# A hybrid encoder trunk on one core: projection groups computed by halves of the tokens, and the differential rotation done by VectorE's shuffle

## The reference, cut to what matters

```python
def apply_partial_rope(x, cos, sin):
    r = cos.shape[-1]                       # 8 of a head's 64 features
    x1, x2, rest = x[..., :r], x[..., r:2 * r], x[..., 2 * r:]
    return jnp.concatenate([x1 * c - x2 * s, x2 * c + x1 * s, rest], axis=-1)

def diff_mixer(q, k, v, ...):
    q = apply_partial_rope(rms_norm(q.reshape(b, t, 8, 64), q_head_g), cos, sin)
    k = apply_partial_rope(rms_norm(k.reshape(b, t, 8, 64), k_head_g), cos, sin)
...
    u = rms_norm(h, attn_norm_g[l]) @ w_in[l]      # 40 groups of 128 columns
```

## Time and profile before

| | |
|---|---|
| median of 3 runs | 2256.19 us (2255.35 to 2264.37) |
| the profiled execution, its own time | 2260.73 us |
| its span, first to last instruction | 2258.9 us |
| mean granted TensorE clock | 0.975 |
| TensorE matmul busy | 2062.5 us (91%) |
| VectorE, ScalarE, GpSimd busy | 1063.1, 820.8, 993.5 us |

### The profile page before, as it was taken

One profiled execution on the slowest core, in us unless ns is written; L12 is line 12 of the kernel. 1 busy time (PEld: TensorE's weight loads), 2 busy tenths in 40 slices (PEclk: granted clock), 3 DMA queues, 4 the chain that ended last, 5 costly groups with the idle time before them and its releaser, 6 DMA issues.

```text
span 2258.9 us, 32608 instructions
## 1 busy us (share of the span) xinstructions
PE 2062.5 (91%) x13298; PEld 1781.2 (79%) x13298; DVE 1063.1 (47%) x1653; ACT 820.8 (36%) x1344; POOL 993.5 (44%) x593
## 2 busy tenths in 40 slices
PE   7989998888778999999999999997877789999999
PEld 7978887567657999999989878884555567888887
DVE  8532355565664744442038332555655656444400
ACT  3322343576554222222224322443664633222221
POOL 4455432784311444444434454335861334444444
PEclk9999999999998999999999999999998999999999
DMA  4211111000001222233222111111000012333333
GB/s 161 66 56 57 57 46 67 10 1 19 29 12 37 85 94 87 91 94 94 94 85 84 57 57 57 48 38 56 1 7 31 19 56 94 94 94 98 97 103 112
DMA packets 40035, 143.79 MB, mean 64 GB/s; under 512 B 4432, under 2 KB 4560, under 8 KB 39760
## 3 DMA queue, kind: packets, MB, share of 16 engines
q1 hardware_dynamic: 39888, 141.72, 19.6%
HBM read 139.60 MB, written 2.10 MB: 63 GB/s over the span
## 4 chain that ended last, share of the span: by engine, by line
PE 72%; DVE 11%; ACT 8%; issue 6%; POOL 2%; DMA 1%; SPq 0%; ACTq 0%; DVEq 0%; POOLq 0%
PE pb L850 44%; PE pb L885 6%; PE pb L886 6%; PE pb L887 6%; ACT ebuf L1468 2%; PE pb L1287 1%; DVE rowmax L1926 1%; POOL parts L632 1%; PE pb L1295 1%; ACT rstd L1436 1%; PE pb L1227 1%; DVE proj L1858 1%; PE pb L987 1%; ACT ebuf L1479 1%; ACT parts L1524 1%
## 5 line engine op out<-in xcount | busy, mean ns | idle before, releaser
L632 POOL TENSOR_TENSOR parts<-raw,parts 128x1024 fp32r<-128x1024 f32 x248 | 602.5, 2430 | 829.0 <-ACT parts L1524 828.8
L850 PE MATMUL pb<-mix,parts 128*128 128x264 f32 x4608 | 670.7, 294 | 41.1 <-POOL parts L632 15.7
L850 PEld LDWEIGHTS pb<-mix,parts 128*128 128x128 f32 x4608 | 609.2, 193 | 68.0 <-issue 26.1
L1524 ACT ACTIVATE parts<-raw 128x1024 fp32r<-128x1024 f32 x248 | 262.5, 1058 | 851.1 <-PE pb L850 549.6
L850 PE MATMUL pb<-proj_r,parts 128*128 128x264 f32 x3104 | 429.2, 286 | 0.5 <-POOL parts L632 0.5
L850 PEld LDWEIGHTS pb<-proj_r,parts 128*128 128x128 f32 x3104 | 401.2, 189 | 0.8 <-issue 0.7
L885 PE MATMUL pb<-proj_r,parts 128*128 128x512 f32 x528 | 207.5, 393 | 0.8 <-DVE mbuf L1858 0.8
L887 PE MATMUL pb<-proj_r,parts 128*128 128x512 f32 x528 | 207.7, 393 | 0.0
L886 PE MATMUL pb<-proj_r,parts 128*128 128x512 f32 x496 | 198.1, 399 | 0.0
L1864 DVE TENSOR_TENSOR h<-h,pb 128x528 f32<-128x528 f32 (+1 forms) x48 | 33.2, 693 | 274.9 <-PE pb L850 143.9
L1858 DVE TENSOR_TENSOR mbuf<-pb,rstd 128x528 f32<-128x528 f32 (+1 forms) x44 | 30.8, 700 | 214.8 <-PE pb L850 110.5
(11 more groups left out here) (277 smaller groups left out, 2831.6 us busy)
## 6 DMA issues: line engine op xcount, KB each, us to landing
raw<-w_stream SPq DMA_DIRECT2D x250, 512.0 KB, 3.5
w_head<-w_heads SPq DMA_DIRECT2D x8, 512.0 KB, 4.9
h<-x_t SPq DMA_DIRECT2D x8, 264.0 KB, 6.8
out_t<-h SPq DMA_DIRECT2D x8, 256.0 KB, 4.7
con<-consts SPq DMA_DIRECT2D x1, 1652.5 KB, 10.5
par<-params SPq DMA_DIRECT2D x1, 340.0 KB, 4.3
con<-consts SPq DMA_DIRECT2D x1, 128.0 KB, 7.1
```

Source lines behind the costliest of these rows:

```text
L632: nc.gpsimd.tensor_tensor(parts[:, n % PARTS, 1, :], w, parts[:, n % PARTS, 0, :].bitcast(FP32), ALU.subtract).then_inc(split.sem, 1)
L850: last = nc.tensor.matmul(pb[rows_, 2 * p + a, 0:HALF], lhs_t, rhs[:, a * HALF:(a + 1) * HALF], start=start, stop=stop)
L1524: nc.scalar.activation(parts[:, n % PARTS, 0, :], raw[:, r % RAW, :], ACT.Copy).then_inc(lead_ready.sem, 1)
```

## The change

Both parts touch slots 0 to 99 alone, in both layers.

By halves: a group's 48 matmuls keep their number, but the 24 of the first half of the tokens come first (slots 4n, 4n+1), then the 24 of the second (4n+2, 4n+3). VectorE scales each half out by its own instruction (128x264): the first at slot 4n+2, ahead of that slot's jobs, the second at the next boundary. A boundary's first piece waits for the first half of the group before, slot 4n+2 for its second.

Rotation: `perm_d` is no longer multiplied. At the norm's slot VectorE shuffles the scaled tile into `BM` (`stream_shuffle`, 32 partitions at a time, the first two eights swapped). At `turned` it multiplies `BM` by the sines in place, and the sum with GpSimd's cosine product comes at the next slot, as the job `roped`. The sign goes into the sine table once, at group 6 of layer 0.

```diff
+TURNED_AT = ((1, 64), (2, 68), (3, 72), (4, 76), (6, 82), (7, 86), (9, 92), (10, 97))
-               + [(slot, "turned", j) for j, slot in ((1, 64), (2, 68), ...])
+               + [(slot, "turned", j) for j, slot in TURNED_AT] + [(slot + 1, "roped", j) for j, slot in TURNED_AT])
...
 GpSimd, cosines
-                pool.wait_ge(rs_used.sem, rs_used.at(l, j + 1))
-                pool.wait_ge(rot_ready.sem, rot_ready.at(l, t + 1))
+                pool.wait_ge(swapped.sem, swapped.at(l, t + 1))
...
 TensorE
+            def half_piece(l, g, a, k0):
+                n = l * N_SLOT + g
+                if k0 == 0 and a == 0:
+                    pe.wait_ge(split.sem, n + 1)
+                    if g == G_SSD:
+                        pe.wait_ge(evac.sem, evac.at(l, g))
+                    else:
+                        pe.wait_ge(half_evac.sem, half_evac.at(l, g - G_SSD))
+                elif k0 == 0:
+                    pe.wait_ge(evac.sem, evac.at(l, g))
+                o, cut = pb[:, 2 * bank_pair(g) + a, 0:HALF], slice(a * HALF, (a + 1) * HALF)
+                for k in range(k0, k0 + KD // 2):
+                    w_lead, w_rest = (parts[:, n % PARTS, b, k * P:(k + 1) * P] for b in range(2))
+                    lead, rest = (ap[:, cut] for ap in xg_parts(k))
+                    nc.tensor.matmul(o, w_lead, lead, start=(k == 0), stop=False)
+                    nc.tensor.matmul(o, w_lead, rest, start=False, stop=False)
+                    last = nc.tensor.matmul(o, w_rest, lead, start=False, stop=(k == KD - 1))
+                if k0:
+                    done = w_used if a else half_done
+                    last.then_inc(done.sem, 1)
...
-            def turned(l, j):
-                pe.wait_ge(log_ready.sem, log_ready.at(l, RS_N + j + 1))
-                pe.wait_ge(rs_used.sem, rs_used.at(l, j + 1))
-                product(2, C("perm_d"), tile_of(proj, DQ + NORMS[j][1]), True, True).then_inc(rot_ready.sem, 1)
...
-                    k = (KD // PIECES) * (p % PIECES)
-                    beside(l, G_SSD + p // PIECES, 0, xg_parts, ((k, k + KD // PIECES),))
+                    half_piece(l, G_SSD + p // PIECES, p % PIECES // 2, KD // 2 * (p % 2))
...
 VectorE, norm
+                if what == "d":
+                    dve.wait_ge(rs_used.sem, rs_used.at(l, j + 1))
+                    dve.wait_ge(roped.sem, roped.at(l, t))
+                    nc.vector.stream_shuffle(tile_of(proj, BM), tile_of(proj, tile), SWAP).then_inc(swapped.sem, 1)
 VectorE, turned
-                nc.vector.tensor_tensor(halves(sines), pair(2), halves(C("sin_d")), ALU.mult).then_inc(rot_used.sem, 1)
+                link(nc.vector.tensor_tensor(sines, sines, C("sin_d"), ALU.mult))
+            def sines_added(l, j):
                 dve.wait_ge(qcos.sem, qcos.at(l, t + 1))
+                nc.vector.tensor_tensor(tile_of(proj, DQ + t), tile_of(proj, DQ + t), tile_of(proj, BM), ALU.add).then_inc(roped.sem, 1)
...
                     if p % PIECES == 0 and p:
-                        scale_out(l, g, tile_of(proj, TILE_AT[g]))
+                        scale_half(l, g, 1, tile_of(proj, TILE_AT[g]))
+                    if p % PIECES == 2:
+                        g = G_SSD + p // PIECES
+                        scale_half(l, g, 0, tile_of(proj, TILE_AT[g]))
```

More of the change, by code:

```diff
@@ L62 @@
 N_GROUP = G_FOUT + KD
+SWAP = [*range(DIFF_ROPE // 2, DIFF_ROPE), *range(DIFF_ROPE // 2), *range(DIFF_ROPE, 32)]
 PIECES = 4
@@ L473, in trunk @@
         evac = signal("evac", N_GROUP)
+        half_done = signal("half_done", N_IN - G_SSD)
+        half_evac = signal("half_evac", N_IN - G_SSD)
         xg_ready = signal("xg_ready", 2 * KD)
@@ L539, in trunk @@
         o_ready = signal("o_ready", NT)
-        rot_ready = signal("rot_ready", 8)
-        rot_used = signal("rot_used", 8)
+        swapped = signal("swapped", 8)
+        signed = signal("signed", 0)
         roped = signal("roped", 8 + 2 * MLA_H)
@@ L1171, in ml_job @@
                     norm(l, n)
-                elif what == "turned":
-                    turned(l, n)
             for l in range(DEPTH):
@@ L1858, in scale_out, with scale_half @@
                 nc.vector.tensor_tensor(of_group(l, g, dst), group_sum(l, g), of_group(l, g, rstd[:, :]), ALU.mult).then_inc(evac.sem, 1)
+            def scale_half(l, g, a, dst):
+                cut = slice(a * HALF, (a + 1) * HALF)
+                if a:
+                    dve.wait_ge(w_used.sem, w_used.at(l, g + 1))
+                else:
+                    dve.wait_ge(half_done.sem, half_done.at(l, g - G_SSD + 1))
+                ins = nc.vector.tensor_tensor(dst[:, cut], pb[:, 2 * bank_pair(g) + a, 0:HALF], rstd[:, cut], ALU.mult)
+                released = evac if a else half_evac
+                ins.then_inc(released.sem, 1)
             def residual(l, g, k):
@@ L1992, in column_table, with sine_signs @@
                 nc.vector.tensor_copy(lin2[32:32 + NDEC, :], C("lin_sp", slice(0, NDEC))[:, C_DT:C_DT + NDEC]).then_inc(lin_ready.sem, 1)
+            def sine_signs():
+                link(nc.vector.reduce_sum(rowmax[:, 0:1], C("perm_d"), axis=AX.X))
+                nc.vector.tensor_scalar(C("sin_d"), C("sin_d"), rowmax[:, 0:1], -1.0, ALU.mult, ALU.mult).then_inc(signed.sem, 1)
             def decays(l):
@@ L2167, in turned @@
                 sines = tile_of(proj, BM)
-                dve.wait_ge(rot_ready.sem, rot_ready.at(l, t + 1))
-                nc.vector.tensor_tensor(halves(sines), pair(2), halves(C("sin_d")), ALU.mult).then_inc(rot_used.sem, 1)
-                dve.wait_ge(rot_used.sem, rot_used.at(l, t + 1))
+                dve.wait_ge(swapped.sem, swapped.at(l, t + 1))
+                dve.wait_ge(signed.sem, 1)
+                link(nc.vector.tensor_tensor(sines, sines, C("sin_d"), ALU.mult))
+            def sines_added(l, j):
+                t = NORMS[j][1]
                 dve.wait_ge(qcos.sem, qcos.at(l, t + 1))
-                nc.vector.tensor_tensor(tile_of(proj, DQ + t), tile_of(proj, DQ + t), sines, ALU.add).then_inc(roped.sem, 1)
+                nc.vector.tensor_tensor(tile_of(proj, DQ + t), tile_of(proj, DQ + t), tile_of(proj, BM), ALU.add).then_inc(roped.sem, 1)
             def ml_job(l, what, n):
@@ L2189, in ml_job @@
                     turned(l, n)
+                elif what == "roped":
+                    sines_added(l, n)
             nc.vector.memset(eps[:, :], EPS).then_inc(eps_ready.sem, 1)
@@ L2225, in _ @@
                             column_table()
+                            sine_signs()
                     if g == MISC + 2:
```

6 lines of the change are left out of this document (1 added, 5 removed).

## The result

| | before | after |
|---|---|---|
| median of the runs | 2258.82 us | **2227.45 us** (2227.13 to 2231.24, 4 runs) |
| ratio | | **0.987**, 95% interval 0.9845 to 0.9895 |
| span of the profiled execution | 2258.9 us | 2225.7 us |
| slots 0 to 99, layer 0 and layer 1 | 255.8, 249.5 us | 235.1, 235.1 us |

A forecast was written before the change was run, and what follows sets the result against it. TensorE, busy 91% of the span, was taken as the bound. Layer 0's terms, 6.3 + 7.3 + 2.9 + 2.0 = 18.5 us, and layer 1's 17.7 make 36.2: 2256.2 - 36.2 = 2220 us, range 2212 to 2236.

The forecast's parts named there:

- the return at slot 88: Norm 8's sum at slot 88: TensorE arrives while VectorE still adds squares, so 0.4 us of the saving comes back.
- Part 1: Group boundaries: TensorE's waits for scale-outs go with token halves, 6.3 us a layer, 0.28 of it at slot 4.
- Slot 4: Longest scale-out wait, layer 0: stays, VectorE being late with eight small copies; only the shorter scale-out gains, 0.28 us.
- Part 2: Permutation products leave TensorE: seven of a layer's eight gain 6.2 us, the scaled tile's wait 1.1; sum 7.3.
- Part 3: Norm 5's sum at slot 78: squares' addition moves ahead of the rotation's sum; 2.9 us gained, 0.5 of wait stays.
- Part 4: Lower granted clock after slot 78's stall: 2.0 us lost in layer 0, 1.2 in layer 1, neither expected afterwards.
- what would make it wrong: Slow piece matmuls, shuffles over 2 us, new VectorE waits at slots 73 to 94, clock falling at slot 94 instead.
- Eaten at slot 94: Slot 94's wait for ScalarE's square grows by what slots 88 to 92 save (eighth product, 0.88 us, and its boundary).
- VectorE's new work: Eight shuffles a layer at 0.7 us, 5.6 us on an engine with 150 us idle; sine product up to 1.7 more.
- The banks: Rival: twelve matmuls in a row into one bank make each matmul slower; 0.05 over 0.5% slower, 0.02 near no change.
- the chain takes over: Rival: VectorE, ScalarE and GpSimd, not TensorE, set the pace from slot 60 on; 2229 to 2242 us, chance 0.22.

The follow-up runs named there:

- experiment 4: The changed kernel with four of ScalarE's squares ahead of the mLSTM step or the norm in ScalarE's program: 2228.85 us, ratio 0.9868 to the kernel before.
- experiment 2: The changed kernel with groups in quarters of K over both token halves, as before, so only the rotation is new: 2259.27 us, ratio 0.9995 to the kernel before.
- experiment 7: The changed kernel with cosine product, ScalarE's squares and some additions earlier, shuffle a slot later, decay copies in slot 5: 2212.48 us, ratio 0.9798 to the kernel before.
- experiment 5: The changed kernel with each of the 16 shuffles issued twice, one after the other: 2241.35 us, ratio 0.9922 to the kernel before.
- experiment 6: The changed kernel with VectorE's eight small copies of the decays in slot 5 instead of slot 0: 2228.4 us, ratio 0.9863 to the kernel before.

## Why the prediction was right, step by step

The sign and the size were right, and its largest terms are in the traces. Part of the size is luck: the slots gave 35.1 us for 36.2 counted, but 5.9 of them came at slot 4, where 0.6 was counted. The other terms gave 29.2 us where 35.6 were counted: the return at slot 88 cost 3.0 more, slot 78 gave 2.5 less, the clock's fall at slot 94 cost 2.7, and the rest gave a little more than counted. And two large terms hang on each other, which the sum did not show.

- **Part 1, boundaries.** 6.05 us a layer for the boundaries other than slot 4. The halves alone gave 6.3 at slots 24 to 96 in layer 0 by the same comparison of starts. Right.
- **Slot 4** was to give 0.28 and gave 5.65 in layer 0 (0.2 in layer 1). The copies ahead of the scale-out were short in this execution (1.2 us at most, against 2.38), so the wait of 4.5 was 0.65 and no clock fell behind it. The change has little part in it: with the rotation alone, whose scale-outs are those of before, 3.9 us of it came as well, and the copies were short in every other trace that has them at slot 0. The step took one long case for the rule; layer 1 of the kernel before, with 2.4 us between the pieces there, would have shown that it was none. Why the copies ran long stood in the trace of before, right beside the copy of 2.38 us (132.49 to 134.87):

```profile
132.47 2.37 POOL L632 TENSOR_TENSOR parts<-raw,parts 128x1024 fp32r<-128x1024 f32 x1
```

  Each long copy there lasted until a GpSimd operation ended. In layer 1, and in the other traces with the copies at slot 0, every second copy fell into a gap between two such operations and took 0.15 us.
- **Part 2, the permutation product.** 0.86 to 0.90 us came back at slots 68, 82, 92 and 97, where nothing hides it, and 2.1 at slot 86 (0.88 + 1.1 predicted). But the return at slot 88, counted at 0.4, was 1.7 (the wait) to 1.9 us: the shuffle ahead of the addition of squares took 0.76, and the cosine product held the addition for 0.8. That GpSimd holds VectorE's operations was in the text for the sine product; it was not applied to the addition.
- **Part 3, slot 78.** 2.9 counted, 1.85 and 1.45 measured: a wait of 1.5 stayed, where 0.5 was expected. Most of it is the square that came behind ScalarE's scaling: with that square early (experiment 4) the wait was gone. The hold (1.20 instead of 0.69 us beside L779) is 0.5 of it.
- **Part 4, the clock.** 1.9 and 1.2 us at slots 78 and 79, as counted. But "with the stall gone I expect neither" holds for this place only: the clock fell at slot 94 instead and cost 1.4 us a layer there, which the text had named as what would make it wrong. So had it named new waits for VectorE at slots 73 to 94, and the one at 88 came.
- **Eaten at slot 94.** The wait is 1.9 us instead of 1.0, the product's 0.88 was eaten as said.
- **VectorE's new work.** The shuffle took 754 ns, near the lower bound chosen. The Trainium skill (VectorE: DVE Perf Modes, the perf-mode tier table) led to an estimate of 0.62 us; the measurement decides. The half scale-out took 0.43 as read off the line through two rows. The sine product took 0.70 in the median and up to 2.87.
- **The banks.** 12 matmuls into one bank start within 1.33 to 1.34 us (slots 71 and 97 of layer 0) against 1.35 for the two banks in turn (slot 71 before): no price. That rival is out.

In sum (the 0.88 of slot 92 eaten at 94) layer 0 got 5.65 + 6.3 + 6.3 (8.2 less the 1.9 at slot 88) + 1.85 + 1.9, less 1.4: 20.6 us, layer 1 14.2, against 20.7 and 14.4 measured. Without the luck at slot 4 the profiled executions would lie about 5 us less apart; whether the medians would, no trace shows.

What the sum hid: it reads as if part 2 could be had alone. It can't (experiment 2). The rival "the chain takes over" was the right worry. It was priced with TensorE's waits of the kernel before, in which the permutation products and boundary waits still kept TensorE slow enough for VectorE's chain. In the changed kernel that chain is level with TensorE from slot 74 on: one more 0.76 us ahead of the split costs 5 us at slot 78, and the reordering of experiment 7 gained 15 us without taking any work away. The 150 us of idle time on which the forecast leaned were no measure of that.

## What to carry to other kernels

When an engine is made faster, price each saving with the other savings already made: run the change's parts alone in the head, each against the waits it uncovers, since parts may be worth nothing alone and everything together. Look in every stretch for what stands between an operation that may be held (here a sum that waits for another engine) and the instruction that the bottleneck needs next, and move that instruction ahead, or let it be needed later. Idle time of a helper engine in sum says nothing; its slack is at the place where its program meets another engine's long operation, and a fix at one place is worth judging only with those behind it.

## What the runs showed of the hardware

VectorE's operations with two inputs in SBUF did not run beside GpSimd's: in five cases from four kernels they ended 0.55 to 0.57 us after GpSimd's operation did (the addition at 303.94 + 2.39 = 306.33 and 304.13 + 2.76 = 306.89; 343.95 and 344.51; 341.12 and 341.67; in the changed kernel 331.77 and 332.34, 308.94 and 309.51). An operation of 128x4 elements was held as well (2.04 us). Counted over all twelve traces, 470 such operations started more than 0.1 us inside a GpSimd operation on two tensors of over 0.9 us, and 468 ended behind it; the other two (0.69 us each, rotation alone) ran while GpSimd's own operation was drawn out (2.54 instead of 1.30 us). So the holding goes both ways: in the changed kernel the cosine product that began at 308.90, during the addition, took 1.77 us.

One input is enough for it in copies and casts from SBUF: all 606 of those, counted in the same way, ended behind GpSimd's operation, the copies at slot 4 among them. With one input in PSUM it is otherwise. The sine product of the kernel before ran its usual time inside a weight split, and by moving it to SBUF the change made it one that can be held (2.87 us):

```profile
284.88 2.39 POOL L632 TENSOR_TENSOR parts<-raw,parts 128x1024 fp32r<-128x1024 f32 x1 [6.21 <-ACT parts L1524]
285.05 0.71 DVE L2169 TENSOR_TENSOR proj<-pb,con 128x528 f32<-128x528 f32 x1 [0.65 <-PE pb L850]
```

A shuffle, with one input in SBUF, is not held: in experiment 5 six of them started inside a weight split and took 745 to 774 ns, the first of them here:

```profile
283.35 2.40 POOL L636 TENSOR_TENSOR parts<-raw,parts 128x1024 fp32r<-128x1024 f32 x1 [4.50 <-ACT parts L1537]
```

```profile
283.98 0.77 DVE L2196 STREAM_SHUFFLE proj<-proj 128x528 f32<-128x528 f32 x1
```

The Trainium skill (SBUF — State Buffer, section "SBUF: two separate sides") calls the port pair that both engines share an exclusive lock, in which the later one blocks; the traces agree, for operations with two inputs.

How much of a stall is the holding can be read from these rows: about 2 of 4.0 us at slot 88 of experiment 2, 0.5 and 0.8 us at slots 78 and 88 of the changed kernel. The rest is waiting in order behind another engine. No kernel was run in which GpSimd's splits were away, so that the stalls would go with them is argued only.

The clock fell at slot 94 of the changed kernel behind a wait of 1.89 us (granted clock 0.60 in the next 4 us). In experiment 6 the same wait of 1.89 us at the same slot of layer 0 had no fall behind it, and in layer 1 a later one. So the wait alone does not decide it; what else does is open, and it is worth about 1.4 us at this slot. Shuffling into PSUM, which would take the second SBUF input of the sine product away, was not tried.
